# Expert products with both activation halves in one 512-column matmul, in a two-layer encoder kernel

## What is computed

```
s = queries x sub_keys, top 16 per side and head -> idx, g = softmax(best)
a = gelu(sum_d u_tab[idx, d] * x[t, d])      # 8 heads x 16 picks per token
out[t] = sum_k (g * a)[t, k] * v_tab[idx[t, k], :]
```

## Time and profile before

| | |
|---|---|
| median of 3 runs | 2042.25 us (2041.79 to 2042.98) |
| profiled execution, device time | 2039.95 us |
| its span, first to last instruction | 2038.1 us |
| TensorE matmul busy | 1952.9 us, 96% of the span |
| VectorE, ScalarE, GpSimd busy | 1320.5, 1103.7, 769.7 us |
| mean granted TensorE clock | 0.991 |

### The profile page before, as it was taken

How to read it: one execution, slowest core, us unless ns; L and a number is a source line. 1 busy time by engine, 2 the same in 40 slices (tenths; PEclk the granted TensorE clock), 3 DMA queues, 4 the chain that set the end, 5 groups by cost and what they waited for, 6 DMA issues and landing times.

```text
span 2038.1 us, 43068 instructions
## 1 busy us (share of the span) xinstructions
PE 1952.9 (96%) x12792; PEld 1782.5 (87%) x12792; DVE 1320.5 (65%) x2869; ACT 1103.7 (54%) x2124; POOL 769.7 (38%) x553
## 2 busy tenths in 40 slices
PE   7989998999999999999998999989999999999997
PEld 5779997999999888888777799979999998888886
DVE  4655699566666666666547557986666666666665
ACT  4344454666664555555533454546666555555554
POOL 4433599567770000000064416995767600000000
PEclk9989999999999999999989999999999999999999
DMA  6215454544445567555522154544444456665555
GB/s 210 74 42 172 151 184 138 162 137 141 137 140 172 186 208 246 196 192 191 184 74 83 55 183 148 183 144 145 144 134 144 134 175 196 226 227 194 196 192 179
DMA packets 93499, 327.09 MB, mean 160 GB/s; under 512 B 10736, under 2 KB 11504, under 8 KB 93168
## 3 DMA queue, kind: packets, MB, share of 16 engines
q1 hardware_dynamic: 93424, 326.18, 49.1%
HBM read 325.09 MB, written 1.05 MB: 160 GB/s over the span
## 4 chain that ended last, share of the span: by engine, by line
PE 89%; DVE 5%; issue 3%; POOL 2%; ACT 1%; DMA 0%; DVEq 0%; POOLq 0%; SPq 0%; ACTq 0%
PE ps L820 12%; PE ps L821 12%; PE ps L822 12%; PE ps L893 11%; PE ps L895 11%; PE ps L896 11%; PE ps L839 6%; PE ps L793 2%; PE ps L796 2%; PE ps L795 2%; POOL tab_lo L1264 1%; DVE work L1370 1%; PE ps L604 1%; PE ps L570 1%; PE ps L523 1%
## 5 line engine op out<-in xcount | busy, mean ns | idle before, releaser
L1264 POOL TENSOR_TENSOR tab_lo<-raw,tab_hi 128x512 fp32r<-128x512 f32 x416 | 585.9, 1422 | 262.5 <-ACT tab_hi L1096 181.6
L820 PE MATMUL ps<-x_lo,tab_hi 128*128 128x256 f32 x2048 | 591.8, 289 | 22.2 <-POOL tab_lo L1264 18.9
L822 PE MATMUL ps<-x_hi,tab_lo 128*128 128x256 f32 x2048 | 579.1, 283 | 0.0
L821 PE MATMUL ps<-x_hi,tab_hi 128*128 128x256 f32 x2048 | 579.0, 283 | 0.0
L1677 DVE TENSOR_TENSOR tab_lo<-raw,tab_hi 128x512 fp32r<-128x512 f32 x512 | 354.4, 692 | 268.7 <-ACT tab_hi L1191 265.3
L1096 ACT ACTIVATE tab_hi<-raw 128x512 fp32r<-128x512 f32 x504 | 317.6, 631 | 339.0 <-PE ps L822 334.5
L820 PEld LDWEIGHTS ps<-x_lo,tab_hi 128*128 128x128 f32 x2048 | 392.1, 191 | 25.7 <-POOL tab_lo L1264 25.5
L893 PE MATMUL ps<-tab_lo,w_hi 128*128 128x512 f32 x1024 | 398.6, 389 | 0.9 <-DVE w_lo L1685 0.9
L896 PE MATMUL ps<-tab_hi,w_lo 128*128 128x512 f32 x1024 | 398.4, 389 | 0.0
L895 PE MATMUL ps<-tab_hi,w_hi 128*128 128x512 f32 x1024 | 398.4, 389 | 0.0
L821 PEld LDWEIGHTS ps<-x_hi,tab_hi 128*128 128x128 f32 x2048 | 392.6, 192 | 0.0
(11 more groups left out here) (204 smaller groups left out, 2524.8 us busy)
## 6 DMA issues: line engine op xcount, KB each, us to landing
raw<-tab_u SPq DMA_DIRECT2D x256, 512.0 KB, 3.3
raw<-tab_v SPq DMA_DIRECT2D x256, 512.0 KB, 3.3
raw<-w_proj SPq DMA_DIRECT2D x68, 512.0 KB, 3.6
raw<-w_proj SPq DMA_DIRECT2D x16, 384.0 KB, 3.2
work<-cdft SPq DMA_DIRECT2D x18, 256.0 KB, 3.8
work<-cfilter SPq DMA_DIRECT2D x9, 256.0 KB, 4.3
work<-sub_keys SPq DMA_DIRECT2D x2, 1024.0 KB, 6.5
work<-pmat SPq DMA_DIRECT2D x6, 304.0 KB, 4.4
```

The lines of the kernel that those rows point to most:

```text
L820: mm(bank, hi, x_lo[:, 4 * h + k, :], start=(h + k == 0), stop=False)
L821: mm(bank, hi, x_hi[:, 4 * h + k, :], start=False, stop=False)
L822: last = mm(bank, lo, x_hi[:, 4 * h + k, :], start=False, stop=(h + k == 4))
L1264: tt(half(tab_lo, s, h), half(raw, s, h), half(tab_hi, s, h).bitcast(F32), ALU.subtract).then_inc(lo_pool.sem, 1)
```

## The change

For tiles 48 to 127 of the first table `u_tile_joint` replaces `u_tile`. x_hi and x_lo lie side by side (`x_hl`), and one matmul of 512 columns multiplies tab_hi by both, followed by one of 256 columns for tab_lo by x_hi. Each tile then takes a bank of its own (0 to 3) with two parts, which have to be added. `sum_pair` on VectorE adds them for a pair, with one tensor_reduce over 128x1024 numbers in PSUM into `sums` in SBUF; gelu reads `sums` and writes the first halves of the banks. In `gate_quad` sum_pair takes the place of gate_pair, which moves one tile later; in `tail_quad` sum_pair comes at the even tiles; sum_pair of pair 63 stands ahead of the second table's first lower part. The gate matmuls use banks 4 and 5 only. `iota` is copied to PSUM bank 7 once for each layer (`iota_ps`), and hot_rows and hot_columns read it from there. The region reserved for descriptors of dynamic DMAs is made smaller.

```diff
--- before.py
+++ after.py
 ...
         x = sb("x", [P, TB, D])
-        x_hi = sb("x_hi", [P, DT, SEQ], F32R)
-        x_lo = sb("x_lo", [P, DT, SEQ], F32R)
+        x_hl = sb("x_hl", [P, DT, 2, SEQ], F32R)
         raw = sb("raw", [P, 4, D])
 ...
         dist_abs = sb("dist_abs", [P, 4, P])
+        sums = sb("sums", [P, 2, 2, SEQ])
         ps = ctx.enter_context(nc.psum_tensor("ps", [P, 8, 512], F32))
 
+        x_hi, x_lo = x_hl[:, :, 0, :], x_hl[:, :, 1, :]
         workf = work[:, :, :].rearrange("p j t -> p (j t)")
 ...
         minus_j = chosenf[:, 0:SEQ]
+        iota_ps = ps[:, 7, 0:P]
         place_u = onef[:, 0:256].bitcast(U32).rearrange("p (s n) -> p s n", s=2)
 ...
         unit_set = sig("unit_set", 3)
+        summed = sig("summed", (P - GATE0) // 2)
         gated = sig("gated", (P - GATE0) // 2)
 ...
 
+                def u_tile_joint(i, s, signal, offset):
+
+                    j = i * 4 + s
+                    for h in range(2):
+                        pe.wait_ge(*at(signal, l, j * 2 + offset + h + 1))
+                        for k in range(4):
+                            col = slice(k * P, (k + 1) * P)
+                            hi, lo = half(tab_hi, s, h)[:, col], half(tab_lo, s, h)[:, col]
+                            mm(ps[:, s, :], hi, x_hl[:, 4 * h + k, :, :].rearrange("p a t -> p (a t)"),
+                               start=(h + k == 0), stop=False, skip_group_check=True)
+                            last = mm(ps[:, s, 0:256], lo, x_hi[:, 4 * h + k, :], start=False, stop=(h + k == 4),
+                                      skip_group_check=True)
+                        last.then_inc(half_used.sem, 1)
+
                 def u_product(i, first, signal, offset):
 ...
                     pe.wait_ge(*at((hot_j_act, hot_j_dve)[s % 2], l, i * 2 + s // 2 - GATE0 // 2 + 1))
-                    if not first:
-                        pe.wait_ge(*at(weighted, l, n - 3))
+                    if s >= 2 or not first:
+                        pe.wait_ge(*at(weighted, l, n - 1))
                     for t in range(4):
-                        last = mm(ps[:, 2 + s, t * P:(t + 1) * P], onehot[:, s % 2, 0, t, :],
+                        last = mm(ps[:, 4 + s % 2, t * P:(t + 1) * P], onehot[:, s % 2, 0, t, :],
                                   onehot[:, s % 2, 1, t, :], start=True, stop=True)
 ...
                         if s % 2 == 0:
-                            if first:
-                                pe.wait_ge(*at(gelu_done, l, i * 2 + s // 2 - 1))
-                            else:
+                            if not first:
                                 pe.wait_ge(*at(gated, l, i * 2 + s // 2 - 1 - GATE0 // 2))
-                        u_tile(i, s, lo_pool, LO_G)
+                            elif s == 0:
+                                pe.wait_ge(*at(gelu_done, l, i * 2))
+                        u_tile_joint(i, s, lo_pool, LO_G)
                         gates(i, s, first)
 ...
                             pe.wait_ge(*at(gated, l, i * 2 + s // 2 - 1 - GATE0 // 2))
-                        u_tile(i, s, lo_dve, LO_T)
+                        u_tile_joint(i, s, lo_dve, LO_T)
 
 ...
                 def gelu_in_place(n, bank):
-                    act.wait_ge(*at(half_used, l, n * 4 + 2 * U0 + 4))
-                    fn(ps[:, bank, :], ps[:, bank, :], ACT.Gelu).then_inc(gelu_done.sem, 1)
+                    act.wait_ge(*at(summed, l, n - GATE0 // 2 + 1))
+                    fn(ps[:, 2 * bank:2 * bank + 2, 0:256], sums[:, bank, :, :], ACT.Gelu).then_inc(gelu_done.sem, 1)
 
 ...
                     u_lower(i)
+                v.tensor_copy(iota_ps, iota)
                 dve.wait_ge(*at(picksT_ready, l, 1))
 ...
                     for t in range(4):
-                        last = v.tensor_scalar(onehot[:, slot, 0, t, :], iota, picks[:, 0, bass.ds(n * 4 + t, 1)],
+                        last = v.tensor_scalar(onehot[:, slot, 0, t, :], iota_ps, picks[:, 0, bass.ds(n * 4 + t, 1)],
                                                picks[:, 2, bass.ds(n * 4 + t, 1)], ALU.is_equal, ALU.mult)
 ...
                 def hot_columns(n):
-                    v.tensor_tensor(onehot[:, 1, 1, :, :], iota.rearrange("p (a c) -> p a c", a=1).broadcast_to([P, 4, P]),
+                    v.tensor_tensor(onehot[:, 1, 1, :, :], iota_ps.rearrange("p (a c) -> p a c", a=1).broadcast_to([P, 4, P]),
                                     picks[:, 1, bass.ds(n * 4, 4)].rearrange("p (t a) -> p t a", a=1)
 ...
 
+                def sum_pair(n, bank):
+
+                    dve.wait_ge(*at(half_used, l, n * 4 + 2 * U0 + 4))
+                    v.tensor_reduce(sums[:, bank, :, :],
+                                    ps[:, 2 * bank:2 * bank + 2, :].rearrange("p k (a t) -> p k t a", a=2),
+                                    AX.X, ALU.add).then_inc(summed.sem, 1)
+
                 def gate_pair(n, bank, groups):
 ...
                     pair = work[:, bass.ds(2 * n, 2), :]
-                    v.tensor_tensor(pair, ps[:, bank, :].rearrange("p (k t) -> p k t", k=2), pair, ALU.mult)\
-                        .then_inc(gated.sem, 1)
+                    v.tensor_tensor(pair, ps[:, 2 * bank:2 * bank + 2, 0:256], pair, ALU.mult).then_inc(gated.sem, 1)
 
 ...
                         if s == 0 and not first:
+                            sum_pair(i * 2 - 1, 1)
+                        if s == 1 and not first:
                             gate_pair(i * 2 - 1, 1, n)
 ...
                         if s == 2:
+                            sum_pair(i * 2, 0)
+                        if s == 3:
                             gate_pair(i * 2, 0, n)
 ...
                             u_lower_half(i + 1, 0, 1)
-                        weigh_group(n, 2 + s)
+                        weigh_group(n, 4 + s % 2)
 
 ...
                                 u_lower_half(i, s, h)
-                        if s % 2:
+                        if s % 2 == 0:
+                            sum_pair(i * 2 + s // 2 - 1, (s // 2 + 1) % 2)
+                        else:
                             gate_pair(i * 2 + s // 2 - 1, (s // 2 + 1) % 2, GROUPS)
 ...
                 dve.wait_ge(*at(weighted, l, GROUPS))
+                sum_pair(63, 1)
                 v_quad(0, True)
 ...
 
-    nc = bacc.Bacc("TRN2", target_bir_lowering=False, num_devices=1)
+    nc = bacc.Bacc("TRN2", target_bir_lowering=False, num_devices=1, dynamic_dma_scratch_size=1024)
     arrays = layouts(inputs)
 ...
```

## The result

The changed kernel takes 2055.83 us (median of 4 runs, 2055.2 to 2059.83) against 2042.02 us for the kernel before: ratio 1.0074, 95% interval 1.006 to 1.0088, slower by 13.8 us. The forecast was 2051.8 us, slower, range 2040 to 2061. The profiled execution took 2055.2 us, its span is 2053.1 us. Lines of the code have moved: `u_tile_joint` is L836 and L838, gates L856, hot_rows L1629, hot_columns L1634, weigh_group L1641, sum_pair L1647, gate_pair L1656, gelu L1144, distances L1152, GpSimd's lower part L1281, the second table L910 to L913.

A forecast was written before the change was run, and what follows sets the result against it. TensorE bounds the kernel, but the gate stage's chain through sum_pair and gelu makes it wait. Gates +3.8, tail -1.6, second-table gap +2.6: +4.8 us a layer, +9.6 on 2042.25, giving 2051.8 us; range 2040 to 2061.

The forecast's parts named there:

- TensorE's gain: First table: 512-column matmuls replacing two of 256 save 0.10 us a tile, 16 us for 80 tiles and two layers.
- The chain and its rule: Gate stage: 8.01 us from gates' end through sum_pair and gelu to the pair after next; pair 7.67 us, +3.8 a layer.
- the factor of one half: Gate stage: two periods equal one TensorE pair plus the chain, 2T = 7.33 + 8.01, so T = 7.67 us.
- TensorE would be idle 0.35 us ahead of every other tile: Gate stage: expected sign of the chain, TensorE idle about 0.35 us and released by GpSimd's tab_lo.
- hot_rows out of PSUM: VectorE, gate stage: reading iota from PSUM gives a pitch of 0.325 us, four 1.30 us, with no long first one.
- rival 4: Gate stage: longer chain, from fixed PSUM cost on hot_rows or GpSimd's lower part at 1.56 us; 2059.6 us, chance 0.10.
- The gap at the second table: Second table's start: TensorE stands still 3.03 us for sum_pair(63), two lower parts and w_lo; net +2.6 us a layer.
- the standstill of 3 us could cost clock: After the gap at the second table: 1.2 GHz for some 3.4 us, +1.7 us a layer, counted only in the range.
- the old wait at the second tile: Second table: the earlier 0.43 us TensorE wait at 670.54, which the new standstill replaces.
- Rival 1: Gate stage: the chain has slack and TensorE takes its whole gain; 2031.4 us, chance 0.12.
- Rival 2: Gate stage: break even, hot_rows stay at 0.258 us pitch and gelu at 0.51; 2042.3 us, chance 0.16.
- Rival 3: sum_pair reads its pairs, 1 KB apart, at half rate, 2.29 us; 2086 us, chance 0.05.

The follow-up runs named there:

- after_again: The changed kernel, unaltered, profiled and timed once more: 2055.68 us, ratio 1.0064 to the kernel before.
- upper_first: Changed kernel with ScalarE's gate-stage order altered: distances and upper parts of the next pair's first tile go ahead of the waiting gelu; 2038.46 us, ratio 0.9978.
- sum_first: Changed kernel with sum_pair ahead of hot_rows in VectorE's gate-stage order, ScalarE's order kept; 2038.25 us, ratio 0.9981.
- double_sum: Changed kernel with sum_pair's reduction done twice in the gate stage, the extra result going where nothing is needed; 2089.85 us, ratio 1.0232.
- iota_sbuf: Changed kernel with hot_rows and hot_columns reading iota from SBUF again; 2151.76 us, ratio 1.0533.
- upper_first_late_sum: Changed kernel with ScalarE's upper parts ahead of gelu and the last pair's sum_pair behind the second table's first w_lo; 2029.57 us, ratio 0.9937.
- iota_psum_alone: Kernel before with only iota copied to PSUM and read from there; 2042.76 us, ratio 1.0001.
- late_sum: Changed kernel with the last pair's sum_pair behind w_lo of the second table's first tile, its gelu and gate_pair one tile later; 2047.1 us, ratio 1.0021.
- keep_clock: Changed kernel with 14 dummy float32 matmuls of 128 columns on TensorE in the gap ahead of the second table; 2052.43 us, ratio 1.0054.

## Why the prediction was right, and where it was not

- **TensorE's gain.** Right in kind, too large by about a fifth in the gate stage. The tail tiles took 2.78 us in the profile shown and 2.83 in after_again, upper_first and sum_first, and a pair of the gate stage 7.34 or 7.38 us once nothing waits (7.33 forecast). Why the same matmuls take 0.05 us a tile more in one execution than in another stays open.
- **The chain and its rule.** Right in every link (7.94 us for 8.01) and in what it does to the period: 7.66 us a pair for 7.67, +3.7 us a layer for +3.8. double_sum bears out the factor of one half (0.55 us a pair for 1.13), iota_sbuf too (1.6 for 3.0), upper_first and sum_first that each link on it counts only down to TensorE's own pair. One detail was wrong: I said TensorE would be idle 0.35 us ahead of every other tile. In the second half of the stage it stands still for some 0.6 us ahead of one tile in four, and the turns alternate (gelu at 498.50, 506.61, 513.89, so 8.11 and 7.28 us). The recurrence fixes two turns together and not how they share the wait; the mean is the same.
- **hot_rows out of PSUM.** Right: 402 ns on average, 0.065 above the old 0.337, half of the 0.125 us at twice the columns, so the difference goes with the columns. That no fixed part comes on top shows in hot_columns: 0.68 us with iota in PSUM as with all in SBUF. The fixed cost of a PSUM source in the Trainium skill's errata table (VectorE: DVE Perf Modes, The TRN2 errata), which rival 4 put on top, is not borne out here. By the hot rows alone it would not be excluded: an estimated 0.065 us is also what the table's fixed cost comes to by itself.
- **The gap at the second table.** Right: 3.1 us for 3.03.
- **The step that was mis-sized** is "the standstill of 3 us could cost clock", in the paragraph ahead of the numbers, which stood in the range and not in the sum. It measured 1.6 and 1.4 us in the two layers of the profile shown; +1.7 was the prediction's own figure for it. The term beside it, -0.43 us for the old wait at the second tile, was a little small: in the kernel before the two starts around that wait, 669.72 and 670.54, lie 0.59 us further apart than a pitch, and without half clock the second table takes 348.3 us for 348.9. So its row in the ledger, +1.0, is -0.6 and +1.6. With 3.0 us added, the forecast's +9.6 is +12.6, and the two series gave +13.8 and +13.0. What is left is no more than one run of the changed kernel differs from another (2055.2 to 2059.83 us).
- **Rivals.** Rival 1, TensorE takes its whole gain, is what upper_first, sum_first and upper_first_late_sum make of the change; it needed an order that the change does not have. Rival 2, break even, fell with the hot rows at 0.40 us. Rival 3 fell with sum_pair at 1.21 us: two operands 1 KB apart in PSUM take no longer than the 1.22 us of L1401.
- **A saving priced too low.** I treated the move of iota to PSUM as a loss of 0.27 us in the chain against a small wait. iota_sbuf shows that without it this change would have cost 110 us. No term of the forecast depends on it, since the forecast was for iota in PSUM.

## What to carry to other kernels

When an instruction in the middle of an in-order engine gets a new and later input, list what stands behind it: here a 1.2 us sum, behind other work on an engine that had been busy for 67% of the stage, cost TensorE 9 us a layer, because upper parts for later tiles were queued behind the gelu that waited for it, and moving gelu behind those upper parts gave all of it back. Where a chain runs from the end of one turn's own work to the start of the turn after next, what it has in excess of a turn shows by half, and chain plus turn over two is the period to compute. Look, too, at the last turn of a loop, where there is no other work to hide a new step.

## What was not expected of the hardware

VectorE's tensor_scalar out of SBUF and GpSimd's tensor_tensor exclude each other instruction by instruction: with both engines issuing in a row (iota_sbuf, 507.6 to 512.0), three of the four 0.34 us hot rows took 1.32 us, about the length of one GpSimd instruction, and GpSimd's kept their 1.28 to 1.29 us. This agrees with the exclusive lock that the Trainium skill describes (SBUF — State Buffer, Who interferes with whom). In this stretch it was the VectorE instruction that waited each time; the lower part of 1.56 us in the earlier trace rows says that it can also be GpSimd's. With one operand in PSUM the wait was gone (402 ns on average, GpSimd's at 1.29 us).

A standstill of 3.1 us between two stretches in which TensorE was fully busy brought a half-clock interval in 12 of 14 cases (seven traces with this gap, two layers each); in some it began in the last 0.6 us of the gap. Of the twelve layers of the six traces in which TensorE goes on working there, none had one: not the kernel before (two traces), not iota_psum_alone, late_sum or upper_first_late_sum, and not keep_clock, where dummy matmuls fill the 3.1 us.
